# A two-block transformer step on one core: narrower projections and another order for the gated linear attention of the second block

## The reference

```
u = x * (1 + sc1) + sh1
na_q, na_k, na_v, gl_q, gl_k, gl_v, gl_g, gl_lr, ga_q, ga_k, ga_v = split(u @ w_in)
   # widths 384 384 384 | 128 128 256 256 32 | 384 128 128
la = log_sigmoid(gl_lr(2 x 16) @ wa2(2 x 16 x 128) + ba) / 16       # both directions
o_gl = rms_norm(chunked linear attention(gl_q, gl_k, gl_v, exp(cumsum la))) * silu(gl_g)
o_ga = softmax attention, 6 query heads on 2 key heads, over latent and context keys
o_na = neighbourhood attention, 6 heads, with a bias, over latent and context keys
x = layer_norm(alpha x + g1 * (concat(o_na, o_gl, o_ga) @ w_out))
x = layer_norm(alpha x + g2 * swiglu(...))                          # width 2816
```

## Time and profile before

| | us |
|---|---|
| median of 3 runs | 2316.12 (2315.18 to 2317.22) |
| the profiled execution | 2320.34, span 2318.6 |
| PE busy | 2062.0 |
| ACT busy | 413.7 |
| DVE busy | 544.6 |
| POOL busy | 191.3 |

### The profile page before, as it was taken

One profiled execution on the slowest core, in us unless ns is written; L12 is line 12 of the kernel. 1 busy time (PEld: TensorE's weight loads), 2 busy tenths in 40 slices (PEclk: granted clock), 3 DMA queues, 4 the chain that ended last, 5 costly groups with the idle time before them and its releaser, 6 DMA issues. The chain is left out here.

```text
span 2318.6 us, 33200 instructions
## 1 busy us (share of the span) xinstructions
PE 2062.0 (89%) x14444; PEld 1446.4 (62%) x14444; DVE 544.6 (23%) x1171; ACT 413.7 (18%) x754; POOL 191.3 (8%) x183
## 2 busy tenths in 40 slices
PE   7999889887788789887888877998999999999997
PEld 3756557563346546654456533765888877588886
DVE  5153630012430201000001201356300023731001
ACT  2112112122130200000000310335200024530001
POOL 0520000002000000000000000036000002510000
PEclk9999989998899999999999989999999999999999
DMA  9567989999999999999999999530543842124450
GB/s 368 195 247 285 402 327 416 412 420 424 423 377 426 426 426 421 425 414 421 424 416 426 426 370 419 145 108 1 182 145 111 195 137 92 55 73 157 147 150 18
DMA packets 181192, 664.05 MB, mean 286 GB/s; under 512 B 17335, under 2 KB 123352, under 8 KB 142456
## 3 DMA queue, kind: packets, MB, share of 16 engines
q1 hardware_dynamic: 181048, 661.93, 72.9%
HBM read 660.86 MB, written 1.05 MB: 285 GB/s over the span
## 5 line engine op out<-in xcount | busy, mean ns | idle before, releaser
L1094 PE MATMUL ps<-arena,ring 128*128 128x256 f32 x1984 | 429.1, 380 | 1.8 <-DVEq L390 1.8
L1094 PEld LDWEIGHTS ps<-arena,ring 128*128 128x128 f32 x1984 | 377.5, 190 | 53.1 <-DVEq L390 2.6
L643 PE MATMUL ps<-arena,ring 128*128 128x256 f32 (+2 forms) x1532 | 347.3, 389 | 15.3 <-DMA ring<-in_context_weights 6.5
L643 PEld LDWEIGHTS ps<-arena,ring 128*128 128x128 f32 (+2 forms) x1532 | 275.3, 185 | 94.8 <-issue 30.1
L1473 PE MATMUL ps<-ring,arena 128*32 128x256 f32 x4032 | 259.0, 404 | 84.0 <-DMA ring<-in_w_gate 43.5
L1473 PEld LDWEIGHTS ps<-ring,arena 128*32 128x32 f32 x4032 | 126.4, 115 | 201.5 <-DMA ring<-in_w_up 54.0
L2075 ACT ACTIVATE arena<-ps 128x512 f32<-128x512 f32 (+3 forms) x137 | 74.7, 545 | 788.6 <-PE ps L643 399.5
L1499 PE MATMUL ps<-ring,arena 128*32 128x512 f32 x1024 | 143.1, 687 | 61.2 <-DMA ring<-in_w_down_slots 55.2
L1499 PEld LDWEIGHTS ps<-ring,arena 128*32 128x32 f32 x1024 | 31.3, 120 | 153.9 <-DMA ring<-in_w_down_slots 88.9
L1170 PE MATMUL ps<-arena,ring 128*128 128x256 f32 x512 | 116.3, 390 | 2.9 <-DMA ring<-in_w_out 2.9
L1170 PEld LDWEIGHTS ps<-arena,ring 128*128 128x128 f32 x512 | 100.2, 197 | 19.5 <-issue 5.6
(11 more groups left out here) (355 smaller groups left out, 1893.4 us busy)
## 6 DMA issues: line engine op xcount, KB each, us to landing
ring<-in_w_up SPq DMA_DIRECT2D x64, 2048.0 KB, 13.6
ring<-in_w_down_slots SPq DMA_DIRECT2D x64, 2048.0 KB, 14.3
ring<-in_w_gate SPq DMA_DIRECT2D x62, 2048.0 KB, 14.1
ring<-in_w_ada SPq DMA_DIRECT2D x36, 2048.0 KB, 11.8
ring<-in_w_ffn_in SPq DMA_DIRECT2D x44, 1024.0 KB, 7.7
ring<-in_context_weights SPq DMA_DIRECT2D x35, 1024.0 KB, 14.6
ring<-in_w_ffn_out SPq DMA_DIRECT2D x16, 1408.0 KB, 7.0
ring<-in_w_in SPq DMA_DIRECT2D x9, 2048.0 KB, 12.0
```

The source lines that it names most:

```text
L643: m = mm(o, a, x, start=(k == 0 and r == 0), stop=(k == kt - 1 and last))
L1094: m = mm(b, w[:, k, c:c + P], src[:, k, :], start=(k == 0), stop=(k == kt - 1))
```

## The change

Four products of the latent mixer are laid out otherwise, and PE's and ACT's orders are rewritten. The context stream keeps its forms.

1. The rank-32 product goes to four groups of output partitions in turn, two of its eight slices each, instead of all eight to the first 32 partitions. `wa2` is repeated four times over the partitions (its DMA grows from 32 to 128 partitions of 2 KB), and z contracts over all 128.
2. The exchanged keys are no longer projected from the weights (16 matmuls). The plain keys are evicted, and two matmuls with the identity (64 x 64 tiles) write them to the other half of the partitions (`keys_swapped`), which ACT evicts again (`gqa_k_swapped`).
3. The values of both attentions are one projection of 512 columns (16 matmuls), from a packed copy of the weights (`w_values_2`); ACT evicts each bank in two pieces.
4. PE's order: rank and gate, z, gl_qk, gl_v, levels 0 and 1, first query bank, level 2, second query bank, level 3, keys, levels 4 and 5, exchanged keys, first head sums, neighbourhood keys with levels 6, 7, 8 in their middle, second head sums, values, head roots.
5. ACT's order: z right behind the gates, the gate logarithms, gl_qk, levels 0 and 1, queries' decay, gl_v, levels 2 to 5, then the first query bank, `upper`, second query bank, squares, level 6, keys, level 7, exchanged keys, squares, head roots, neighbourhood keys, values.

```diff
+            part |= {"ga_k": cols(wi, 2336, P), "nv": I["w_values_2"][l].rearrange("(k p) n -> p k n", p=P)}
-            stream += part("na_q", "gl_g", "gl_qkv", "ga_q", "ga_kv", "na_k", "na_v", "wo0", "wo1")
+            stream += part("na_q", "gl_g", "gl_qkv", "ga_q", "ga_k", "na_k", "nv", "wo0", "wo1")
+            def rank_and_gate(l, N, banks, turn):
+                w = take("gl_g" + N)
+                b = open_bank(pe, "gl_lr" + N, banks)
+                for k in range(KD):
+                    pe.wait_ge(u_ready[X], KD * turn + k + 1)
+                    c = 32 * (k % 4)
+                    m = mm(b[c:c + 32, 0:T], w[:, k, 2 * P:2 * P + 32], U[:, k, :], start=(k < 4), stop=(k >= 4))
+                close_bank(m, "gl_lr" + N)
+                b = open_bank(pe, "gl_g" + N, banks)
+                for o in range(2):
+                    for k in range(KD):
+                        m = mm(b[:, T * o:T * o + T], w[:, k, P * o:P * o + P], U[:, k, :], start=(k == 0), stop=(k == KD - 1))
...
-                    m = mm(b[:, T * d:T * d + T], wa2[0:32, l, d, :], gllr[0:32, :], start=True, stop=True)
+                    m = mm(b[:, T * d:T * d + T], wa2[r, l, d, :], gllr[r, :], start=True, stop=True)
...
+                if N[0] == "x":
+                    return project("ga_k" + N, [("ga_k" + N, [features(0, 0)])], banks, parts, between=between)
...
+            def keys_swapped(l, N, banks):
+                bank, use = place["ga_k" + N]
+                pe.wait_ge(free[bank], use + 1)
+                b = open_bank(pe, "ks" + N, banks)
+                for i in range(2):
+                    r, o = slice(64 * i, 64 * i + 64), slice(64 - 64 * i, 128 - 64 * i)
+                    m = mm(b[o, 0:T], ident[r, r], gak[r, 0, kslice(X, l)], start=True, stop=True)
+                close_bank(m, "ks" + N)
...
-                spec = [(f"na_v{t}{N}", [tokens(0, 0, 384, t)]) for t in range(2)]
-                return project("na_v" + N, spec, banks, parts)
+                spec = [(f"na_v{t}{N}", [tokens(0, 0, 512, t)]) for t in range(2)]
+                return project("nv" + N, spec, banks, parts)
...
-                whole(gates(X, l, N, bk, 2 * l))
+                rank_and_gate(l, N, bk, 2 * l)
                 forget_gates(X, l, N, bk)
                 whole(gla(X, l, N, bk))
-                whole(gqa_q(N, bk))
-                whole(gqa_kv(N, bk, between={"ga_k" + N: lambda: levels(0, 1, 2)}))
+                levels(0, 1)
+                whole(gqa_q(N, bk, between={"ga_q0" + N: lambda: levels(2)}))
                 levels(3)
+                whole(gqa_kv(N, bk))
+                levels(4, 5)
+                keys_swapped(l, N, bk)
                 head_sums(X, N, bk, 0, 3 * l + 2)
+                whole(na_qk("k", N, bk, between={"na_k0" + N: lambda: levels(6, 7, 8)}))
                 head_sums(X, N, bk, 1, 3 * l + 3)
-                levels(4)
-                whole(na_qk("k", N, bk, between={"na_k0" + N: lambda: levels(5, 6)}))
-                levels(7, 8)
                 whole(na_v(N, bk))
...
                 gates(X, l, N)
-                gla(X, l, N)
+                forget_gates(X, l, N)
                 gate_logs(X, l)
-                gqa_q(X, N)
+                evac("gl_qk" + N, glqk[:, 0, :], n=T, frees=False, scale=32 ** -0.5)
+                evac("gl_qk" + N, glqk[:, 1, :], o=T, n=T)
                 level(0, X, 1 + l)
                 level(1, X, 1 + l)
                 act.wait_ge(sums_ready[X], l + 1)
                 step(a(qe, B_x, ACT.Exp), qe_exp)
+                evac("gl_v" + N, glv)
+                for n in range(2, 6):
+                    level(n, X, 1 + l)
+                evac("ga_q0" + N, gaq[:, 0:2, :])
+                upper(X, N)
+                evac("ga_q1" + N, gaq[:, 2, :], n=T)
+                gqa_q_squares(X)
+                level(6, X, 1 + l)
                 gqa_k(X, l, N)
+                level(7, X, 1 + l)
+                gqa_k_swapped(l, N)
                 gqa_k_squares(X, l)
...
-                    sp.dma_start(wa2[0:32], I["gla_wa2"]).then_inc(s_tab2, 16)
+                    sp.dma_start(wa2, I["gla_wa2"]).then_inc(s_tab2, 16)
```

More of the change, by code:

```diff
@@ L655, in whole @@
                     assert False
+            def rank_and_gate(l, N, banks, turn):
[10 more added lines that the diff above has]
+                        m = mm(b[:, T * o:T * o + T], w[:, k, P * o:P * o + P], U[:, k, :], start=(k == 0), stop=(k == KD - 1))
+                close_bank(m, "gl_g" + N)
+                release_with("gl_g" + N)
             def gates(st, l, N, banks, turn, parts=1):
-                if st == X or l == 0:
+                if l == 0:
                     spec = [("gl_lr" + N, [features(0, 2 * P, 32)]), ("gl_g" + N, [features(0, 0), features(T, P)])]
@@ L666, in forget_gates @@
                 b = open_bank(pe, "z" + N, banks)
+                r = slice(0, P if st == X else 32)
                 for d in range(2):
-                    m = mm(b[:, T * d:T * d + T], wa2[0:32, l, d, :], gllr[0:32, :], start=True, stop=True)
+                    m = mm(b[:, T * d:T * d + T], wa2[r, l, d, :], gllr[r, :], start=True, stop=True)
                 close_bank(m, "z" + N)
@@ L692, in na_kv, with gqa_q @@
                 return project("na_kv" + N, spec, banks, 4)
-            def gqa_q(N, banks, parts=1):
+            def gqa_q(N, banks, parts=1, between={}):
                 spec = [("ga_q0" + N, [features(0, 0), features(T, P)]), ("ga_q1" + N, [features(0, 2 * P)])]
-                return project("ga_q" + N, spec, banks, parts)
+                return project("ga_q" + N, spec, banks, parts, between=between)
             def gqa_kv(N, banks, parts=1, between={}):
+                if N[0] == "x":
+                    return project("ga_k" + N, [("ga_k" + N, [features(0, 0)])], banks, parts, between=between)
                 spec = [("ga_k" + N, [features(0, 0), swapped(T, 0, 0), swapped(T, 0, 1)]),
@@ L2080, in gates @@
             def gates(st, l, N):
-                evac("gl_lr" + N, gllr[0:32, :], n=T, width=32)
+                r = P if st == X else 32
+                evac("gl_lr" + N, gllr[0:r, :], n=T, width=r)
                 tell(lr_ready[st])
@@ L2089, in gla @@
                 evac("gl_qk" + N, glqk[:, 1, :], o=T, n=T)
[L2090 to L2093, removed]
+                if l == 1:
+                    forget_gates(st, l, N)
                 evac("gl_v" + N, glv)
@@ L2115, in gqa_k, with gqa_k_swapped @@
             def gqa_k(st, l, N):
-                evac("ga_k" + N, gak[:, :, kslice(st, l)])
+                if st == X:
+                    evac("ga_k" + N, gak[:, 0, kslice(st, l)], n=T)
+                else:
+                    evac("ga_k" + N, gak[:, :, kslice(st, l)])
+            def gqa_k_swapped(l, N):
+                evac("ks" + N, gak[:, 1, kslice(X, l)], n=T)
             def gqa_v(st, l, N):
@@ L2120, in gqa_v, with both_values @@
                 evac("ga_v" + N, gav[:, t:t + 2, :], n=T)
+            def both_values(l, N):
+                for t in range(2):
+                    evac(f"na_v{t}{N}", nav[:, vtile(X, l) + t, :], n=384, frees=False)
+                    evac(f"na_v{t}{N}", gav[:, vtile(X, l) + t, :], o=384, n=P)
+                tell(kv_ready)
             def gqa_k_squares(st, l):
@@ L2333, in latent @@
                 step(a(qe, B_x, ACT.Exp), qe_exp)
+                evac("gl_v" + N, glv)
[6 more added lines that the diff above has]
+                level(6, X, 1 + l)
                 gqa_k(X, l, N)
-                level(2, X, 1 + l)
-                gqa_q_squares(X)
+                level(7, X, 1 + l)
+                gqa_k_swapped(l, N)
                 gqa_k_squares(X, l)
[L2338 to L2343, removed]
                 for q in range(2):
                     head_roots(X, N, q)
-                level(7, X, 1 + l)
                 na_k(X, l, N)
-                na_v(X, l, N)
+                both_values(l, N)
                 gla_squares(X, 1 + l)
@@ L2918, in _ @@
                     sp.dma_start(arena[:, 0:n_tab2], I["tables2"]).then_inc(s_tab2, 16)
-                    sp.dma_start(wa2[0:32], I["gla_wa2"]).then_inc(s_tab2, 16)
+                    sp.dma_start(wa2, I["gla_wa2"]).then_inc(s_tab2, 16)
                     sp.dma_start(tab[:, 2 * P:2 * P + n_tab3], I["tables3"]).then_inc(s_tab2, 16)
-                if stream[n][0] in ("ga_kvx0", "na_qx1"):
+                if stream[n][0] in ("ga_kx0", "na_qx1"):
                     l = int(stream[n][0][-1])
@@ L2974, in kernel_arrays @@
     wa = np.stack([np.pad(w[:, d], ((0, 0), (16 * d, 16 - 16 * d), (0, 0))) for d in range(2)], 1)
-    a["gla_wa2"] = np.ascontiguousarray(wa.transpose(2, 0, 1, 3))
+    a["gla_wa2"] = np.ascontiguousarray(np.tile(wa.transpose(2, 0, 1, 3), (4, 1, 1, 1)))
     blocks = [np.asarray(i[key])[l].reshape(-1, P, np.asarray(i[key]).shape[2])[k:k + kt, :, c0:c0 + w].transpose(1, 0, 2).reshape(-1)
@@ L2981, in kernel_arrays @@
```

(2 more changed lines are left out.)

## The result

The changed kernel takes 2300.16 us (median of 4 runs, 2294.27 to 2302.04), the kernel before 2316.67 (4 runs, 2315.18 to 2317.72). The ratio is 0.9925, 95% interval 0.9905 to 0.9945. Forecast were 2292.0, range 2287 to 2301. The direction and the range hold, the range by 0.8 us, but a third of the forecast gain of 24.1 us is missing. The profiled execution is the fastest of the four, 2294.27 with a span of 2292.5.

A forecast was written before the change was run, and what follows sets the result against it. TensorE's work and waits were taken to bound the latent mixers. Per layer 2.5 + 5.4 + 1.9 - 0.4 (seams) + 2.9 = 12.3 us; two layers 24.6, less 0.5 for wa2, 24.1: from 2316.12 to 2292.0 us, range 2287 to 2301.

The forecast's parts named there:

- A: Mixer: a level is late after all, at 0, 1 or level 3's banks; 2 us a layer, 2296; chance 0.17.
- Rival B: Rank product and exchanged keys: narrow tiles don't overlap; 2.7 us a layer come back, 2297.4; chance 0.07.
- Rival C: Attention's start: DVE's diagonal blocks end last and swallow gain, overrunning the margin by 3 us; 2298; chance 0.07.
- Rival E: Ahead of level 0: a further 1.4 us at each table switch, a 2.5 us wait a layer; 2297; chance 0.03.
- The rank product: Mixer, part 1: 16 records on four groups of output partitions run four at a time; gain 2.5 us a layer.
- The exchanged keys: Mixer, part 2: projection replaced by four records taking 0.9 us; gain 5.4 us a layer.
- The values: Mixer, part 3: 32 records of 512 columns take 14.03 us instead of 15.93; gain 1.9 us a layer.
- The waits for POOL: Mixer, parts 4 and 5: TensorE never waits for a level; gain 2.9 us a layer, bounds 0.5 and 2.9.
- Late next: Behind the second head sums: root, reciprocal and diagonal blocks finish 4.2 us before the linear attention's output needs them.
- The sum of a mixer: Gates to head roots: 12.3 us less per layer, 71.7 us in layer 0 and 71.3 in layer 1.
- Behind the mixers: After the head roots: both traces alike, only shifted, so attention and feed-forward give nothing back.
- Rival D: Mixer: levels stay where they were, TensorE waits 18.5 us at level 0; about 2332, slower; chance 0.04.

The follow-up runs named there:

- e1: The changed kernel once more, unaltered: 2302.3 us, ratio 0.9936.
- e3: The changed kernel with parts 1 to 3 undone, the new orders of TensorE and ScalarE kept: 2311.9 us, ratio 0.9983.
- e2: The changed kernel with level 8 moved behind the second bank of neighbourhood keys: 2294.63 us, ratio 0.9904.
- e5: The changed kernel with a one-column exponent behind the second head root, loading the exponent's table early: 2302.44 us, ratio 0.9954.
- e4: The changed kernel with parts 1 to 3 kept and the orders of before restored as far as possible: 2317.36 us, ratio 0.9999.
- e6: On top of e2 (level 8 apart), level 7's small matmuls issued twice: 2299.06 us, ratio 0.9930.
- e8: The changed kernel with never more than two levels in a row and the exponent's table early: 2293.48 us, ratio 0.9911.
- e7: The changed kernel with level 8 apart and the exponent's table early, both: 2292.17 us, ratio 0.9899.

## Why the prediction was right, and by how much it was not

The range held by little, and partly by luck. The changed kernel's second measurement, 2302.3 us (e1), is outside 2287 to 2301. The upper part of the range was made for rivals A, B, C and E, and none of them happened; other losses filled it. And one of the prediction's own signs of being wrong came: "if the attention or the feed-forward part gives part of it back". It gave back 2.2 us. The other sign, a mixer shrinking by less than 9 us, stayed out by little in the first profile (9.18 and 9.90) and came in one mixer of e1 (9.01 and 8.94).

*What bounds it.* Right. The mixers' time is TensorE's, and what TensorE was spared came off the end.

*The rank product.* Forecast: gates to z 9.8 us. Measured 9.66 and 9.50. Four column groups overlap; at the low clock the 16 records end after 1.74 us. z itself came out 0.2 us shorter than before. Rival B is out.

*The exchanged keys.* Forecast 0.9 us for the two small matmuls, measured 0.58 (1500.25 to 1500.83): the two quadrants run side by side. No wait for the eviction.

*The values.* Forecast 14.03 us, measured 13.93. But the gain put down to them, 1.9 us, was mis-sized. The price of 0.169 us a record for 128 columns, which the prediction noted as far above half of 0.216, was the lower clock (e3). At the full clock the two projections take 3.77 + 10.52 = 14.29 us, and joining them gives 0.4. The other 1.6 belong to the waits: a wait of 2 us costs its length and the slow spell behind it. The sum came out right because the two mistakes cancel.

*The waits for POOL.* All gone, as forecast. The margin was thinner than worked out: POOL began 22.0 us behind the gates (1479.55), forecast 21.4, and ended level 1 at 1482.69, just as TensorE came for it (forecast margin 0.7).

*Late next.* DVE's diagonal blocks ended at 1530.2, and the output of the linear attention began at 1534.81: a margin of 4.6 us, forecast 4.2. Rival C did not happen in that form.

*The sum of a mixer.* Forecast 71.7 and 71.3 us. With the holes taken out (e2) they are 71.15 and 71.27. The changed kernel has 74.83 and 73.73 (75.00 and 74.69 the second time). The step that failed is "if TensorE never waits for a level, 2.9 us go", with only semaphores looked at: levels in a row brought a new stall without any, 2.1 and 2.5 us in the two mixers, and behind the first again a slow spell. The spell shows in the 5.18 us of the key records; in layer 1 they take 3.72. The prediction named no such case.

*Behind the mixers.* "Both traces alike, shifted" failed by 2.2 us between the mixers. The change moved all level exponents ahead of the head roots; before, level 7's exponent stood behind them and left its table in place for the softmax. The load of 1.28 us lengthens TensorE's wait by 0.64 us; e5 shows that. The other 1.6 us are the slow spell. It came behind this wait in four of the five profiles with the table late, and some 40 us later in two of the four with it early, so what brings it stays open.

*Rival E.* The rule of the Trainium skill ("ScalarE: Activation LUTs", What ACT_TABLE_LOAD costs) of a drain of some 1.4 us on top of a load is not borne out by the rows here either. In the changed kernel the table load starts at 1541.71, lasts 1.28 us, and the exponent behind it began at 1543.01; ahead of level 0, where the rival saw the cost, the load starts at 1477.48 and the exponent at 1478.78.

*Rival D.* It did not happen. But e4 shows that kind of loss: near the orders of before, all that the narrower products save (9.8 us a mixer by the forecast) turns into waits and slow clock.

Of the 24.1 us forecast, 16.5 came. The missing 7.6 are, from the stretches: 3.1 and 2.4 us in the mixers, 2.2 between, 0.3 in the rest, together 8.0. The forecast had taken 0.5 us off for wa2, which these stretches don't hold; that is the difference.

## What to carry to other kernels

Narrower matmuls and a new order were worth 0 and 5 us alone and 16 us together: before work that covers another engine's hops is cut, those hops have to be moved ahead. Ask of every regrouping also how many instructions a microsecond it makes an engine read, and which activation table it leaves behind. When a row's price per column looks odd, look at the clock of that stretch before a gain is built on it.

## What was not expected of the hardware

TensorE stopped for 0.6 to 2.2 us with no semaphore in the place, 13 times in the mixers of eleven profiles: 12 times inside rows of 32 x 32 tiles (384 matmuls and loads in three levels, some 11 ns a record), once in the projection behind them. Its instructions arrive in 16.4 KB packets, and each stop ended 1.2 to 1.6 us after one had landed. All 13 stood at three levels in a row or at levels 4 and 5 with level 3 just ahead; taking level 8 out of its row removed the stops there in every such profile. But no border can be given: layer 0 of e3 and layer 1 of e6 have three levels in a row and no stop, and two pairs 3.7 us apart had none in the kernel before and in e8.

A stop or wait of about 2 us was followed by a spell at half the clock (0.50), worth about another 1.6 us, in some profiles (the kernel before behind 2.00 us, the changed kernel behind 2.08 and 2.49) and not in others (1.90 in the changed kernel, 1.94 and 2.15 in e5, 2.49 in e3). e7 had one behind a stop of 1.54 us.
